# First gate product behind the key products in the gated delta stage, and first merge weights in four pieces

## The reference

```
# gated delta, per head, chunks of 64, forward and backward
a_low = where(strict, (kb k^T) * gam, 0)
t_inv = solve_triangular(a_low + I, I)      # unit lower triangular
u = t_inv @ vb ; w = t_inv @ (kb * exp(dec)) ; then a scan over chunks

# the projection has eight parts; the last two are the gates
... gate_a, gate_b = split(rmsnorm(h) @ w_in)
merged = sigmoid(gate_a) * (y_a @ w_ssd_out) + sigmoid(gate_b) * (y_b @ w_gdn_out)
h = h + merged @ w_out
```

## Time and profile before

| what | us |
|---|---|
| median of three runs (2479.23 to 2486.51) | 2479.97 |
| the profiled execution | 2484.61 |
| its span, first to last instruction | 2482.8 |
| TensorE busy | 2313.3 (93%) |
| VectorE busy | 1521.3 (61%) |
| GpSimd busy | 1235.8 (50%) |
| ScalarE busy | 862.4 (35%) |
| mean granted TensorE clock | 0.966 of 2.4 GHz |

### The profile page before, as it was taken

One profiled execution on the slowest core, in us unless ns is written; L12 is line 12 of the kernel. 1 busy time (PEld: TensorE's weight loads), 2 busy tenths in 40 slices (PEclk: granted clock), 3 DMA queues, 4 the chain that ended last, 5 costly groups with the idle time before them and its releaser, 6 DMA issues. The chain is left out here.

```text
span 2482.8 us, 31792 instructions
## 1 busy us (share of the span) xinstructions
PE 2313.3 (93%) x10852; PEld 1898.2 (76%) x10852; DVE 1521.3 (61%) x3492; ACT 862.4 (35%) x1268; POOL 1235.8 (50%) x983
## 2 busy tenths in 40 slices
PE   7999789788987998898999999999989999999977
PEld 5888478677876887687888888888878888888864
DVE  4443488466672533108887887885228888888833
ACT  5443433234332432322333333333223333333322
POOL 3343086455553333221656666665547665555511
PEclk9999899899998999999999999999999999999989
DMA  3221011033334231303444444446449999999720
GB/s 141 102 87 65 8 49 41 28 128 118 127 118 173 99 119 51 119 34 132 140 140 140 140 145 129 155 144 208 140 135 387 397 366 355 351 350 350 301 102 34
DMA packets 158548, 393.98 MB, mean 159 GB/s; under 512 B 26256, under 2 KB 91920, under 8 KB 147600
## 3 DMA queue, kind: packets, MB, share of 16 engines
q1 hardware_dynamic: 123664, 325.79, 37.5%
q0 software_dynamic: 34816, 67.41, 7.2%
HBM read 327.92 MB, written 65.21 MB: 158 GB/s over the span
## 5 line engine op out<-in xcount | busy, mean ns | idle before, releaser
L1632 POOL DMA_INDIRECT g_dense<-up_gates_summed_sb,up_gate_at_sb x384 | 422.1, 1099 | 316.3 <-issue 221.1
L178 PE MATMUL ps<-n_high_sb,up_u_high_sb 128*128 128x512 f32 x1024 | 405.1, 396 | 7.8 <-DVE up_u_low_sb L1500 7.8
L180 PE MATMUL ps<-n_high_sb,up_u_low_sb 128*128 128x512 f32 x1024 | 404.7, 395 | 0.1
L179 PE MATMUL ps<-n_low_sb,up_u_high_sb 128*128 128x512 f32 x1024 | 404.8, 395 | 0.0
L1833 PE MATMUL ps<-down_v_high_sb,down_w_high_sb 128*128 128x512 f32 x768 | 299.9, 390 | 7.6 <-DVE down_w_low_sb L1783 7.6
L1834 PE MATMUL ps<-down_v_low_sb,down_w_high_sb 128*128 128x512 f32 x768 | 299.7, 390 | 0.0
L1835 PE MATMUL ps<-down_v_high_sb,down_w_low_sb 128*128 128x512 f32 x768 | 299.6, 390 | 0.0
L1500 DVE TENSOR_TENSOR up_u_low_sb<-up_u_sb,up_u_high_sb 128x1024 fp32r<-128x1024 f32 x128 | 156.4, 1222 | 175.7 <-ACT up_u_high_sb L1653 158.8
L1741 ACT ACTIVATE down_v_high_sb<-down_v_sb 128x1024 fp32r<-128x1024 f32 x128 | 134.1, 1048 | 324.2 <-PE ps L1835 290.4
L178 PEld LDWEIGHTS ps<-n_high_sb,up_u_high_sb 128*128 128x128 f32 x1024 | 192.9, 188 | 54.3 <-DVE up_u_low_sb L1500 7.9
L179 PEld LDWEIGHTS ps<-n_low_sb,up_u_high_sb 128*128 128x128 f32 x1024 | 193.0, 188 | 46.0
(11 more groups left out here) (322 smaller groups left out, 4739.1 us busy)
## 6 DMA issues: line engine op xcount, KB each, us to landing
up_u_sb<-expert_u SPq DMA_DIRECT2D x128, 512.0 KB
down_v_sb<-expert_v SPq DMA_DIRECT2D x32, 2048.0 KB
a_dense<-up_gelu_sb SPq DMA_DIRECT2D x128, 256.0 KB
g_dense<-nought_sb SPq DMA_DIRECT2D x8, 3072.0 KB, 10.4
down_gelu_sb<-a_dense SPq DMA_DIRECT2D x32, 768.0 KB
down_gates_sb<-g_dense SPq DMA_DIRECT2D x32, 768.0 KB
w_slots_sb<-w_conv SPq DMA_DIRECT2D x20, 1024.0 KB
merge_slots_sb<-w_gates SPq DMA_DIRECT2D x8, 1024.0 KB
```

The source lines that it names most:

```text
L178: pe.matmul(out, ah, bh, start=k == 0, stop=False)
L179: pe.matmul(out, ah, bl, start=False, stop=False)
L180: last = pe.matmul(out, al, bh, start=False, stop=k == n - 1)
L1632: pool.indirect_dma_start(cells, at, summed[:, tt, k:k + 1], None).then_inc(stored[tt], 16)
```

## The change

In the gated delta stage product 0 is moved as a block. 21 of its 24 matmuls (`AHEAD`) stand right behind the key products, the last three behind the transposes of level 0; levels 1 and 2 have no gate matmuls left. Product 1 keeps its places. The high split of product 0 is ahead of the exponentials on ScalarE, the low split at the head of the trip on VectorE. The order of transfers on SyncE is the same.

In the merge stage the first half chunk is loaded as four pieces of 128x512, each with a semaphore of its own. ScalarE splits them one by one, VectorE (not GpSimd) makes the low halves (`low_pieces`), and TensorE waits for each piece in the first of its four output banks. All later half chunks go as before, with the counts of the semaphores shifted by one.

```diff
@@ gdn_stage, ScalarE
                     last.then_inc(staged[u], 1)
+                side.high(act, i, 0)
                 for u in U:
                     act.wait_ge(summed[u], i + 2)
                     act.activation(e[u][:, :, :], whole4(u), ACT.Exp).then_inc(decayed[u], 1)
-                side.high(act, i, 0)
@@ VectorE
+                side.low(dve, i, 0)
                 for u in U:
                     dve.wait_ge(masked[u], i + 1)
...
                     dve.tensor_tensor(invs[u][:, :, :], pair(sq(m, "eye")), am[u], ALU.subtract).then_inc(inv_done[u], 1)
-                side.low(dve, i, 0)
@@ TensorE, behind the key products (AHEAD = 21)
                     last.then_inc(kq_done[u], 1)
+                side.pe(pe, i, 0, 0, AHEAD)
@@ TensorE, in the levels
-                    if lv != 3:
-                        side.pe(pe, i, lv // 3, 9 * (lv % 3) - 3 * (lv // 3), 9 * (lv % 3) - 3 * (lv // 3) + 3)
+                    if lv == 0:
+                        side.pe(pe, i, 0, AHEAD, 3 * KT)
+                    if lv > 3:
+                        side.pe(pe, i, 1, 9 * (lv - 3) - 3, 9 * (lv - 3))
...
-                    side.pe(pe, i, lv // 3, 9 * (lv % 3) - 3 * (lv // 3) + 3, 9 * (lv % 3) - 3 * (lv // 3) + 6)
+                    if lv > 2:
+                        side.pe(pe, i, 1, 9 * (lv - 3), 9 * (lv - 3) + 3)
...
-                    if lv != 2:
-                        side.pe(pe, i, lv // 3, 9 * (lv % 3) - 3 * (lv // 3) + 6, 9 * (lv % 3) - 3 * (lv // 3) + 9)
+                    if lv > 2:
+                        side.pe(pe, i, 1, 9 * (lv - 3) + 3, 9 * (lv - 3) + 6)
@@ Stream, with whole = 1 if pieces else 0
+            if n < self.whole:
+                for k in range(KT // 2):
+                    sp.dma_start(self.w[:, 0, k, :], self.chunks[0][:, k * CW:(k + 1) * CW]).then_inc(self.piece_in[k], 16)
+                continue
+            if n >= 2 and n - 2 < self.whole:
+                sp.wait_ge(self.piece_low, KT // 2)
...
+        if n < self.whole:
+            for k in range(KT // 2):
+                act.wait_ge(self.piece_in[k], 16)
+                act.activation(self.wh[:, 0, k, :], self.w[:, 0, k, :], ACT.Copy).then_inc(self.piece_high, 1)
+            return
...
+    def low_pieces(self, dve):
+        for k in range(KT // 2):
+            dve.wait_ge(self.piece_high, k + 1)
+            dve.tensor_tensor(self.wl[:, 0, k, :], self.w[:, 0, k, :], bits32(self.wh[:, 0, k, :]), ALU.subtract).then_inc(self.piece_low, 1)
...
+                        if pieces:
+                            pe.wait_ge(self.piece_low, k + 1)
@@ merge_stage, VectorE
             st.done(dve.memset(ss[:, :, :, :], 1.0))
+            stream.low_pieces(dve)
             reduce(1, 0)
```

More of the change, by code:

```diff
@@ L850, in gdn_stage @@
     side = SideGates(m, "gdn", KT)
+    AHEAD = 21
     first = (0, 3)
@@ L1110, with __init__ @@
 class Stream:
-    def __init__(self, m, raw, split, tag, chunks):
-        self.m, self.chunks = m, chunks
+    def __init__(self, m, raw, split, tag, chunks, pieces=False):
+        self.m, self.chunks, self.whole = m, chunks, 1 if pieces else 0
         self.w = raw.take(f"{tag}_slots", [P, 2, KT // 2, CW])
@@ L1121, in __init__ @@
         self.high_done, self.low_done, self.used, self.prod = (m.sem(f"{tag}_{x}") for x in ("high", "low", "first_half_used", "products"))
+        if pieces:
+            self.piece_in = [m.sem(f"{tag}_piece{k}_loaded") for k in range(KT // 2)]
+            self.piece_high, self.piece_low = m.sem(f"{tag}_piece_high"), m.sem(f"{tag}_piece_low")
     def sp(self, sp, others=lambda n: None):
@@ L1135, in high @@
         j, pair = n % 2, n // 2
-        act.wait_ge(self.loaded[j], 16 * (pair + 1))
+        if n < self.whole:
[3 more added lines that the diff above has]
+            return
+        act.wait_ge(self.loaded[j], 16 * (pair + 1 - (0 if j else self.whole)))
         if pair:
@@ L1140, in high @@
         act.activation(self.wh[:, j, :, :], self.w[:, j, :, :], ACT.Copy).then_inc(self.high_done, 1)
+    def low_pieces(self, dve):
+        for k in range(KT // 2):
+            dve.wait_ge(self.piece_high, k + 1)
+            dve.tensor_tensor(self.wl[:, 0, k, :], self.w[:, 0, k, :], bits32(self.wh[:, 0, k, :]), ALU.subtract).then_inc(self.piece_low, 1)
     def pool(self, pool):
-        for n in range(2 * len(self.chunks)):
+        for n in range(self.whole, 2 * len(self.chunks)):
             j = n % 2
-            pool.wait_ge(self.high_done, n + 1)
+            pool.wait_ge(self.high_done, n + 1 - self.whole)
             pool.tensor_tensor(self.wl[:, j, :, :], self.w[:, j, :, :], bits32(self.wh[:, j, :, :]),
@@ L1159, in pe @@
         for j in range(2):
-            pe.wait_ge(self.low_done, 2 * pair + j + 1)
+            pieces = 2 * pair + j < self.whole
+            if not pieces:
+                pe.wait_ge(self.low_done, 2 * pair + j + 1 - self.whole)
             for f in range(4):
@@ L1200, in merge_stage @@
     ss = r.take("mixer_stat", [P, 2, TT, 8])
-    stream = Stream(m, r, r, "merge", chunks)
+    stream = Stream(m, r, r, "merge", chunks, pieces=True)
     prod = stream.prod
```

4 lines of the change are left out of this document (2 added, 2 removed).

## The result

The changed kernel takes 2453.53 us (median of 4 runs, 2451.42 to 2457.01), the kernel before beside it 2481.45 us (2479.23 to 2486.51): ratio 0.9881, interval 0.9866 to 0.9895. The forecast was 2450, its range 2441 to 2463. The profiled execution has a span of 2450.0 us at a mean granted clock of 0.979 of 2.4 GHz, where before had 2482.8 at 0.966.

The account below looks back on a forecast made before the run. TensorE bounds the kernel, so edits pay only where it idles: 5.5 us per trip, 22 over four, plus 7.7 in merge make 30 off 2484.6, giving 2454.6; adjusted to the median of runs, 2450, range 2441 to 2463.

Parts of the forecast that it names:

- VectorE's chain 0.57 us earlier: Head of a trip: with ScalarE's gate split moved, VectorE's chain starts 0.57 us earlier, first inverse near 544.05.
- The low split leaves its place: Between inverses and first parts: moving VectorE's low split saves 1.67 us; with the earlier chain, first parts 2.24 us earlier.
- Level 1: Gated delta level 1 loses three gate groups: 6.54 us becomes 5.5, gain 1.0, ends 0 and 1.4.
- VectorE and GpSimd hold levels 1 and 2: Rival: these levels keep their old length, a trip gains 3.5 us, kernel at 2458; chance 0.15.
- Level 2: Gated delta level 2, with the second low split, 7.20 us before: gain at most 0.77, taken 0.5.
- The clock: Per trip: gates keep TensorE at work, but a clock fall after the level 0 transposes is possible; -0.3 us, ends 0 and -0.9.
- item 3: Gated delta level 0: 7.90 us becomes 5.8, gain 2.1, including y products at full clock, 1.95 for 2.90 us.
- the gates at 1.2 GHz: Rival: the 21 gates take 9.7 us in a 5.07 us hole, delaying the transposes; 2463, chance 0.08.
- the slower rival: Levels 0 to 2 without gates leave TensorE resting, clock stays at 1.2 GHz from the head on; 2496, chance 0.03.
- 0.65, 0.7 and 0.15: Merge start: ScalarE's split of a piece (0.5 to 0.65 us), VectorE's low half (0.7), handing over (0.15).
- pieces land singly: Rival: merge weight pieces land some 1.5 us apart, slower than used; merge gains about 5 us, 2453, chance 0.08.

Follow-up runs that it names:

- masks_halved: Changed kernel with each of GpSimd's four first masks (128x512) made in two halves (128x256): 2456.14 us, ratio 0.9894 to the kernel before.
- second_narrow: Changed kernel with GpSimd's second parts made for half of the columns only, so not a complete computation: 2447.03 us, ratio 0.9863 to the kernel before.
- hole_empty: Changed kernel with the 21 gate matmuls behind the key products left out, not computed: 2455.77 us, ratio 0.9887 to the kernel before.
- both_again: The changed kernel once more, timed beside its two halves on one chip: 2456.5 us, ratio 0.9901 to the kernel before.
- gates_only: Changed kernel with only the gated delta part; the merge stage loads, splits and waits as before: 2463.0 us, ratio 0.9928 to the kernel before.
- pieces_only: Kernel before with the merge part of the change alone, gated delta stage as before: 2474.11 us, ratio 0.9962 to the kernel before.
- second_spread: Changed kernel with product 1 in levels 1 to 4, two groups each, its split behind level 0: 2458.35 us, ratio 0.9903 to the kernel before.
- two_groups_early: Changed kernel with product 1's split behind level 0, one group in levels 1 and 2, two in 3 to 5: 2453.76 us, ratio 0.9884 to before.

## Why the prediction was right, and where it was off

The forecast (2450 for 2453.5) rests on the right mechanisms; by the trace the sum was 5 us too large (30 for 25), 3.5 in the gated delta stage and 1 in the merge. That the number came so near is in part luck: the medians moved by 26.6 to 27.9 us and not by 25, and no run settles where the other 2 to 3 come from.

1. VectorE's chain 0.57 us earlier. The start came as said: L973 follows the key products' start by 1.67 us, 2.25 before. The gain was then lost at once: the copy L977 took 1.12 us for 0.42, beside GpSimd's mask of the last lane. Key products to first inverse is 8.35 (8.22 before). The step failed where it let VectorE start earlier without asking what GpSimd does in that time: worth -0.13, not 0.57. `masks_halved` shows the holding.
2. The low split leaves its place: 4.61 us from the first inverse to the first parts became 2.94, the 1.67 of the forecast exactly. Together 1.54 for 2.24.
3. Level 0: 5.63, forecast 5.8. GpSimd's second parts ended last, as said: at 542.59, and the last lane's product followed at 542.69.
4. Level 1: 6.01, forecast 5.5; gain 0.53 for 1.0. I had VectorE's row at 5.2 to 5.4 with GpSimd closer beside it. Its L992 took 1.1 us longer than before in level 1 (1.82 for 0.75) and 0.5 in level 2 (1.82 for 1.30), and the last inverse came 1.02 us late for TensorE. `second_narrow` (4.81) and `hole_empty` (4.97) show that without GpSimd's backlog the row fits into 5.0. This is the rival "VectorE and GpSimd hold levels 1 and 2", at half its price. By the Trainium skill, page "SBUF — State Buffer", section "Who interferes with whom", VectorE operations with two SBUF inputs and GpSimd operations that read SBUF exclude each other for a whole instruction. The trace agrees. Of the 104 operations of L977, L980, L988 and L992 in the changed kernel, which take both sources from SBUF, 48 took 0.41 to 0.44 us. The other 56 took 0.54 to 1.12, and each of these ended 0.28 or 0.29 us behind the end of a GpSimd operation; before, it was 32 of 104. The 192 of L984 and L996 took 0.41 or 0.42 each, 184 of them with a GpSimd operation beside them; one of their sources is in PSUM.
5. Level 2: 6.99, forecast 6.7; gain 0.21 for 0.5, for the same reason.
6. Levels 3 and 4 are 6.03 and 6.54, and from level 5 to the next key products it is 24.38: unmoved, as said.
7. The clock: 1.00 from the key products into the levels in three trips; in the third it fell at 605.6, behind the last transposes of level 0, and the y products took 3.17 us for 1.95 (levels 6.82, 5.65 and 6.45, 0.3 longer in sum). That is the fall which the item held possible. -0.1 on the mean, forecast -0.3. What I had not priced is what the gates do for the clock, since it stood inside item 3; `hole_empty` puts it at 0.7 us a trip net: 1.6, 2.0, 1.0 and 0.7 in level 0 by trips, less 1.0, 1.0 and 0.7 that level 1 gives back in the first three.

A trip became 4.55 us shorter for 5.5, the stage 18.5 for 22. The chances of the gates at 1.2 GHz and of the slower rival are settled: the gates run at the full clock behind the key products, and the levels keep it in most trips. In the six executions with this stage as changed the clock fell around level 0 in 7 of 24 trips, and no level became longer than before by it.

In the merge stage the first product came 6.6 us earlier in the first trace, 7.0 by `both_again` against `gates_only`; forecast 7.7. From ScalarE's first piece to the first product it is 1.48 us, and the forecast's 0.65, 0.7 and 0.15 make 1.5. The rest is the landing: between 752 and 754 on the time of before I took the middle. 4.95 us after the memset are 754.3 there. The other executions of the changed kernel had 4.02 and 4.05 (753.4), and those of other kernels with the same merge code 3.02 to 4.86 (752.4 to 754.2), so the forecast is met on the average and the 1 us is the spread of this time. No later piece is waited for in the changed kernel, so the rival "pieces land singly" didn't come about, although SyncE issued the four only 0.96 us apart (3.84 us). Something of it appears in `pieces_only` and `second_narrow`: issued in 1.76 us, their second piece kept ScalarE waiting for 1.5 us and TensorE for 0.4. The Trainium skill, page "DMA: Bandwidth & Descriptors", section "Measured (HBM→SBUF, 128 partitions, SWDGE, issued from GpSimd)", advises transfers of 1 MiB or more. Nothing against four parts of 256 KB was felt here: the first was ready after 3.0 to 4.95 us, a whole load after 5.75 to 6.5.

## What to carry to other kernels

Work that hangs on nothing is worth most in the stretch where TensorE waits longest, and it pays there twice: it leaves the place where it stood in the path, and it keeps the clock at 2.4 GHz for most of what comes after. Here the first was worth about 16 us and the second 2.7. Before other groups are moved, look at what is left of TensorE's rest at the place they leave: taking the last one away gave back what the level had won in three trips of four (`second_spread`), leaving one there kept it (`two_groups_early`). Once TensorE's filler is out of a stretch, price the elementwise engines by what they take side by side, not by their lone durations.

## What the runs showed of the hardware

- The clock went to 1.2 GHz behind a rest of 1.76 us but not behind one of 1.27 (`second_spread`), and within one of 5.2 us (`hole_empty`). It stayed at 1.00 through windows with TensorE busy 1.11 and 1.19 of 2.00 us in the second trip of the changed kernel, and fell in the same place in the third.
- Four loads of 256 KB were issued in 1.76 to 3.84 us, and ScalarE's first piece came 3.0 to 4.95 us after the memset, the later the slower the issue; the same kernel had 4.02, 4.05 and 4.95. A load of 1 MB was used after 5.75 to 6.5 us. What decides the issue time isn't settled: it wasn't tried.
- A VectorE operation on 128x256 with both sources in SBUF took 0.41 to 0.44 us, or up to 1.12 where a GpSimd operation was under way; all 56 such long ones of the changed kernel's gated delta stage ended 0.28 or 0.29 us behind a GpSimd operation.
- A 128x2048 low split took VectorE 2.29 us and GpSimd 4.53; in pieces of 128x512 GpSimd took 1.25 each (4.99 for four).
